# Block products over the whole depth in the second MLP product of a hybrid decoder, weight sums on GpSimd

## The reference

```python
hm = rms_norm(x, mlp_norm_g[l]) @ w_mlp1[l]      # 1024 -> 4096
x = x + jnp.square(jax.nn.relu(hm)) @ w_mlp2[l]  # 4096 -> 1024
```

## Time and profile before

| | us |
|---|---|
| median of 3 runs | 3008.79 (3005.19 to 3010.06) |
| the profiled execution | 3007.68 |
| its span, first to last instruction | 3005.6 |
| PE busy | 2824.3 (94%) |
| DVE busy | 1738.5 (58%) |
| POOL busy | 1596.1 (53%) |
| ACT busy | 1129.2 (38%) |
| mean granted clock of TensorE | 0.977 of 2.4 GHz |
| DMA | 208.27 MB, mean 69 GB/s |

### The profile page before, as it was taken

How to read it: one execution, slowest core, us unless ns; L and a number is a source line. 1 busy time by engine, 2 the same in 40 slices (tenths; PEclk the granted TensorE clock), 3 DMA queues, 4 the chain that set the end, 5 groups by cost and what they waited for, 6 DMA issues and landing times.

```text
span 3005.6 us, 33919 instructions
## 1 busy us (share of the span) xinstructions
PE 2824.3 (94%) x12958; PEld 2192.6 (73%) x12958; DVE 1738.5 (58%) x1775; ACT 1129.2 (38%) x1762; POOL 1596.1 (53%) x897
## 2 busy tenths in 40 slices
PE   8999999999999988888999999999999999888887
PEld 6766668887788877666787566788787888766665
DVE  8574465034733357989776644630446333598987
ACT  3455543242433333222215655422414333422233
POOL 4334433422577776666633345234136777766666
PEclk9999999999999999999999999999999999999999
DMA  3100011310133342222110000113011333423221
GB/s 130 47 14 1 15 43 49 106 56 28 45 110 113 113 140 98 70 98 84 56 55 33 14 1 15 56 57 112 29 39 60 109 111 110 146 78 105 70 98 56
DMA packets 96298, 208.27 MB, mean 69 GB/s; under 512 B 11280, under 2 KB 13328, under 8 KB 95504
## 3 DMA queue, kind: packets, MB, share of 16 engines
q1 hardware_dynamic: 96144, 206.18, 20.3%
HBM read 168.13 MB, written 38.01 MB: 69 GB/s over the span
## 4 chain that ended last, share of the span: by engine, by line
PE 65%; DVE 20%; POOL 7%; ACT 3%; issue 2%; DMA 2%; SPq 0%; DVEq 0%; POOLq 0%; ACTq 0%
PE ps L1018 16%; PE ps L1514 12%; PE ps L1588 9%; PE ps L1386 6%; DVE raw_b L2514 6%; DVE b_op L2510 5%; PE ps L1240 4%; POOL ring L887 3%; PE ps L1270 2%; POOL raw L893 2%; PE ps L1442 2%; PE ps L1605 2%; PE ps L1466 2%; PE ps L1256 2%; DVE z L2491 2%
## 5 line engine op out<-in xcount | busy, mean ns | idle before, releaser
L1588 PE MATMUL ps<-b_op,a_op 128*128 128x512 f32 x2352 | 579.8, 409 | 109.0 <-DVE x L2491 59.2
L1588 PEld LDWEIGHTS ps<-b_op,a_op 128*128 128x128 f32 x2352 | 464.8, 199 | 223.7 <-DVE x L2491 64.2
L1018 PE MATMUL ps<-hA,wsp 128*128 128x512 f32 x1920 | 443.1, 392 | 0.1
L721 POOL TENSOR_TENSOR wsp<-raw,ones 128x1024 fp32r<-128x1024 f32 x63 | 125.9, 1999 | 570.8 <-PE ps L1018 454.9
L1018 PEld LDWEIGHTS ps<-hA,wsp 128*128 128x128 f32 x1920 | 360.3, 188 | 80.9 <-issue 6.2
L922 POOL TENSOR_TENSOR a_op<-raw_a,a_op 128x1024 fp32r<-128x1024 f32 x102 | 282.7, 2772 | 224.6 <-ACT a_op L1989 217.0
L887 POOL TENSOR_TENSOR ring<-raw,ring 128x512 fp32r<-128x512 f32 x210 | 272.9, 1299 | 150.4 <-ACT ring L1949 140.9
L1514 PE MATMUL ps<-hT,ring 128*128 128x512 f32 x1440 | 337.3, 394 | 16.1 <-POOL ring L887 16.1
L1514 PEld LDWEIGHTS ps<-hT,ring 128*128 128x128 f32 x1440 | 273.0, 190 | 76.7 <-POOL ring L887 19.5
L1976 ACT ACTIVATE b_op<-raw_b 128x1024 fp32r<-128x1024 f32 x98 | 103.5, 1056 | 424.3 <-DVE raw_b L2514 279.3
L1514 PE MATMUL ps<-hB,ring 128*128 128x512 f32 x1080 | 250.2, 389 | 0.8 <-POOL ring L887 0.8
(11 more groups left out here) (326 smaller groups left out, 4592.4 us busy)
## 6 DMA issues: line engine op xcount, KB each, us to landing
raw<-in_weight_tiles SPq DMA_DIRECT2D x108, 512.0 KB, 3.3
hidden_tiles<-hm_s SPq DMA_DIRECT2D x128, 256.0 KB, 2.0
raw_a<-in_weight_tiles SPq DMA_DIRECT2D x64, 512.0 KB, 3.9
raw_b<-hidden_tiles SPq DMA_DIRECT2D x64, 512.0 KB, 5.4
raw<-in_weight_tiles SPq DMA_DIRECT2D x120, 256.0 KB, 3.1
outT<-x SPq DMA_DIRECT2D x16, 256.0 KB, 2.2
x<-in_xT SPq DMA_DIRECT2D x3, 1024.0 KB, 9.6
wh<-in_head_weights SPq DMA_DIRECT2D x8, 256.0 KB, 2.7
```

What stands on the lines that cost most here:

```text
L721: pool.tensor_tensor(wsp[:, s, 0, :], raw[:, s, :], ones[:, 0:1].to_broadcast([P, TILE]), ALU.mult).then_inc(w_ready[s], 1)
L1018: last = pe.matmul(ps[:, 2 * buf + half, 0:n], w[:, k, col:col + P], rhs(part, k, half * n, n), start=(at_k == 0 and w is w_hi and part == 0),
L1588: last = pe.matmul(ps[:, bank, :], w[:, part, q // 2, r, (q % 2) * P:(q % 2 + 1) * P], h[:, a, r, :], start=(r == 0 and part == 0 and a == ...
```

## The change

The loops of the second MLP product are turned around. A step n is product p = n // 8 and depth block s = n % 8; all eight depth blocks of one product are accumulated in four PSUM banks (M1, M7, M6, M3 in banks 4 to 7, the others in 0 to 3), the eighth block included, so nothing is plain any more and the accumulators `z` are gone. After each product DVE adds its four banks to the blocks of `x` that need it: 13 additions of 4 x 512 elements, and four of 512 after M3. The last two steps of M3 are done unit by unit, from two slots of their own.

The sums of hidden operands are made once, during the first MLP product, by DVE (`pair_sums`, four of 128 x 512 per iteration), and stored to DRAM ready for use: three plain quarters and four sums per pair. The weight operands are loaded anew for each product; eight of M1's stay in `kept_a` and are updated in place. Their sums (M7, M5, M6, M3) are made by POOL (`operand_sum`), one step ahead, between the lows. M5 loads a second weight block (`raw_c`). A weight load is now two transfers with runs of 256 elements. ACT puts two copies ahead of a root at the start of the first MLP product, and `mu` and the `hT` tiles lie elsewhere. Whatever waits are new stand in the diff, cut to its core:

```diff
+STEPS = NFB
+FILLS = NPR * STEPS
+RING_FILLS = FILLS - 2
+OPERAND_SUMS = (P_M7, P_M5, P_M6, P_M3)
...
-        slots = (A, A + 16 * K, A + 48 * K, B + 16 * K)
...
+        slots = (A + 16 * K, A + 48 * K, A, A + 32 * K, B + 8 * K, B + 24 * K)
...
+        raw_c = [at(f"raw_c{n}", B + (24 + 4 * n) * K, [P, 2, HT]) for n in range(4)]
...
+                    def store_sums(f):
+                        for j, p in enumerate((P_M7, P_M5, P_M6, P_M4)):
+                            sp.wait_ge(ht_sum, here(ht_sum, 4 * f + j + 1))
+                            sp.dma_start(hm_d[layer, f, p, :, :], hts[j][:, :]).then_inc(ht_st, 16)
...
+                    def load_weights(n):
+                        p, s = step(n)
+                        rows, parity = {P_M1: (0, 0), P_M2: (0, 1), P_M7: (1, 0), P_M5: (1, 0), P_M6: (1, 1), P_M4: (1, 1),
+                                        P_M3: (0, 1)}[p]
+                        load_block(kept_a[s] if p == P_M1 else raw_a[n % SLOTS], n, rows, parity)
+                        if p == P_M5:
+                            load_block(raw_c[n % SLOTS], n, 1, 1)
...
+                    def load_hidden(n):
+                        p, s = step(n)
+                        sp.dma_start(raw_b[n % SLOTS][:, :, :], hm_d[layer, 2 * s:2 * s + 2, p, :, :].rearrange("r p t -> p r t"))\
+                            .then_inc(ld_b[n % SLOTS], 16)
...
+                            sp.wait_ge(hm_st, here(hm_st, 48 * f))
+                            for n in range(2):
+                                load_weights(n)
+                                load_hidden(n)
+                        store_sums(f - 1)
+                        if more:
...
+                    for n in range(2, SLOTS):
+                        load_weights(n)
+                    sp.wait_ge(hm_st, here(hm_st, 48 * NFP))
+                    for n in range(2, SLOTS):
+                        load_hidden(n)
+                    store_sums(NFP - 1)
+                    sp.wait_ge(c_add, here(c_add, NPR * (NFP - 1)))
+                    for n in range(SLOTS, FILLS):
+                        sp.wait_ge(b_lo, here(b_lo, n - SLOTS + 1))
+                        load_hidden(n)
+                        sp.wait_ge(a_lo, here(a_lo, W1_FILLS + n - SLOTS + 1))
+                        if n == 6:
+                            sp.wait_ge(ht_st, here(ht_st, 64 * NFP))
+                        load_weights(n)
                     if last_layer:
                         sp.dma_start(fin_g[:, :], final_g).then_inc(fin_ld, 16)
...
-                    def a_add(b, n, out, x0, x1, op):
-                        pool.tensor_tensor(raw_a[out][:, :, :], raw_a[x0][:, :, :], raw_a[x1][:, :, :], op).then_inc(a_sum, 1)
...
+                    def operand_sum(n):
+                        p, s = step(n)
+                        pool.wait_ge(blk_ready[n % SLOTS], here(blk_ready[n % SLOTS], W1_LOADS + loads_a(n)))
+                        kept, new = kept_a[s][:, :, :], raw_a[n % SLOTS][:, :, :]
+                        if p == P_M5:
+                            pool.tensor_tensor(new, new, raw_c[n % SLOTS][:, :, :], ALU.add).then_inc(s_sum, 1)
+                            return
+                        pool.wait_ge(a_lo, here(a_lo, W1_FILLS + n - 2 * STEPS + 1))
+                        first, second = (kept, new) if p == P_M7 else (new, kept)
+                        pool.tensor_tensor(kept, first, second, ALU.subtract).then_inc(s_sum, 1)
...
-                    def fold(n, out, x0):
-                        pool.tensor_tensor(out[:, :, :], out[:, :, :], x0[:, :, :], ALU.add).then_inc(fold_z, 1)
...
+                    for n in range(FILLS):
+                        if n + 1 < FILLS and step(n + 1)[0] in OPERAND_SUMS:
+                            operand_sum(n + 1)
+                        operand_low(n)
...
+                    def operand_products(n, q):
+                        p, s = step(n)
+                        w = a_op[op_slot(n)].rearrange("p a c (r m) -> p a c r m", m=2 * P)
+                        h = b_op[op_slot(n)]
+                        for r in range(2):
+                            for part, a in ((0, 0), (0, 1), (1, 0)):
+                                last = pe.matmul(ps[:, 4 * (1 - p % 2) + q, :], w[:, part, q // 2, r, (q % 2) * P:(q % 2 + 1) * P],
+                                                 h[:, a, r, :], start=(s == 0 and r == 0 and part == 0 and a == 0),
+                                                 stop=(s == STEPS - 1 and r == 1 and part == 1))
+                        return last
...
+                    for n in range(RING_FILLS):
+                        p, s = step(n)
+                        operands_ready(n)
+                        if s == 0 and p == 0:
+                            pe.wait_ge(p1_kept, here(p1_kept, NFP - 1))
+                            pe.wait_ge(c_add, here(c_add, NPR * (NFP - 1) - 4))
+                            pe.wait_ge(hm_sq, here(hm_sq, 4 * NFP - 2))
+                        elif s == 0 and p == 1:
+                            pe.wait_ge(hm_sq, here(hm_sq, 4 * NFP))
+                        elif s == 0:
+                            pe.wait_ge(x_add, here(x_add, adds_before(p - 1)))
+                        for q in range(4):
+                            last = operand_products(n, q)
+                        last.then_inc(u_done, 1)
+                    operands_ready(FILLS - 1)
+                    for q in range(4):
+                        if last_layer and q == 2:
                             fin_means(0)
+                        for n in range(RING_FILLS, FILLS):
+                            last = operand_products(n, q)
+                        last.then_inc(u_done, 1)
                     if last_layer:
...
                     def hidden_sq(f, n, bank, k, half):
                         act.wait_ge(hm_t, here(hm_t, 4 * f + n + 1))
                         if f:
-                            act.wait_ge(hm_st, here(hm_st, 64 * f))
+                            act.wait_ge(hm_st, here(hm_st, 48 * f))
+                            act.wait_ge(ht_sum, here(ht_sum, 4 * f))
...
+                    def operands_high(n):
+                        p = step(n)[0]
+                        if n < SLOTS:
+                            act.wait_ge(p_done, here(p_done, NPR * (NFP - 2) + P_M7 + n + 1))
+                        elif n < RING_FILLS:
+                            act.wait_ge(u_done, here(u_done, n - SLOTS + 1))
...
+                    def pair_sums(f):
+                        dve.wait_ge(hm_sq, here(hm_sq, 4 * f + 4))
+                        if f:
+                            dve.wait_ge(ht_st, here(ht_st, 64 * f))
+                        b11, b12, b21, b22 = (hms[k][:, cols_of(half)] for k in range(2) for half in range(2))
+                        dve.tensor_tensor(hts[0][:, :], b22, b12, ALU.subtract).then_inc(ht_sum, 1)
+                        dve.tensor_tensor(hts[1][:, :], b12, b11, ALU.subtract).then_inc(ht_sum, 1)
+                        dve.wait_ge(ht_sum, here(ht_sum, 4 * f + 2))
+                        dve.tensor_tensor(hts[2][:, :], b22, hts[1][:, :], ALU.subtract).then_inc(ht_sum, 1)
+                        dve.wait_ge(ht_sum, here(ht_sum, 4 * f + 3))
+                        dve.tensor_tensor(hts[3][:, :], b21, hts[2][:, :], ALU.subtract).then_inc(ht_sum, 1)
...
-                    def b_sub(b, n, out, x0, x1):
-                        dve.tensor_tensor(raw_b[out][:, :, :], raw_b[x0][:, :, :], raw_b[x1][:, :, :], ALU.subtract).then_inc(b_sum, 1)
...
+                    def operand_low(n):
+                        op = b_op[op_slot(n)]
+                        dve.wait_ge(b_hi, here(b_hi, n + 1))
+                        dve.tensor_tensor(op[:, 1, :, :], raw_b[n % SLOTS][:, :, :], op[:, 0, :, :].bitcast(F32), ALU.subtract)\
                             .then_inc(b_lo, 1)
+                    c11, c12, c21, c22 = (x[:, 4 * (1 - rows):4 * (2 - rows), cols_of(half)] for rows in range(2) for half in range(2))
+                    X_BLOCKS = {P_M1: ((c11, 0), (c12, 0), (c21, 0), (c22, 0)), P_M2: ((c11, 1),), P_M7: ((c21, 3), (c22, 4)),
+                                P_M5: ((c12, 2), (c22, 7)), P_M6: ((c12, 8), (c21, 6), (c22, 9)), P_M4: ((c21, 11),)}
+                    def block_add(p, i):
+                        out, before = X_BLOCKS[p][i]
+                        bank = 4 * (1 - p % 2)
+                        dve.wait_ge(u_done, here(u_done, STEPS * (p + 1)))
+                        if before:
+                            dve.wait_ge(x_add, here(x_add, before))
+                        dve.tensor_tensor(out, ps[:, bank:bank + 4, :], out, ALU.add).then_inc(x_add, 1)
...
-                    def panel_adds(b, p, qs=range(4)):
-                        for q in qs:
-                            out = {P_M1: z1[:, q, :], P_M7: z7[:, q, :], P_M5: z5[:, q, :], P_M6: z6[:, q, :],
-                                   P_M4: x[:, 4 + q, 0:HT], P_M3: x[:, q, HT:T]}[p]
```

(29 more changed lines are left out.)

537 lines of the change are left out of this document (125 added, 412 removed).

## The result

The changed kernel takes 2923.03 us (median of 4 runs, 2921.71 to 2925.76), the kernel before beside it 3007.54 us: a ratio of 0.972, 95% interval 0.9703 to 0.9737. It is 84.5 us faster where 163 were forecast, and above the whole range of 2825 to 2882.

A forecast was written before the change was run, and what follows sets the result against it. VectorE was taken to bound the second MLP product. 3007.68 us less 87.0 (layer 0) and 90.9 (layer 1), plus 15 for the first product and 1.1 for the median, gave 2846; 80% range 2825 to 2882.

The forecast's parts named there:

- What bounds the kernel: The second MLP product is bound by VectorE's in-order list, not TensorE; 85 to 90 us of waits and low clock.
- parts 1 and 2: Second product: 1344 matmuls per layer, 304.7 us; VectorE at most 5.0 us per step against 5.44, so off the path.
- Part 3: Second product: GpSimd's heavy step takes 5.8 us against TensorE's 5.44, covered by four slots; 0 to 3 us per layer.
- Part 4: Between the two MLP products: loads of steps 2 and 3 come slightly late; charged 1 us, bounds 0 and 4.
- Part 5: Second product's loads: no loss per byte, share 0.58, in M5 0.87; 48 more stores at 0.43 us, nothing waiting closely.
- rival 3: Second product: transfers of 1 KB runs at double price, 9 to 20 us per layer, 2864 to 2886; chance 0.07.
- Part 6: First product: VectorE's sums delay M4, 0.45 us per period, 13 us; with the start +15, bounds -6 and +45.
- Rival 2: First product: port turns cost 1.5 us per period, 29 us more, 2875; chance 0.10.
- The start: First product's opening: early copies bring M7 some 3 us forward, sums put M4 back 4; costs 1 us per layer.
- The end: After the last product: four additions, squares and scaling as before, 14.3 us.
- What would be seen: Signs: second product 305 to 311 us, first product's periods 19.4 to 19.6; wrong if a period passes 20 us.
- rival 4: Second product paced by the latency of its loads, slower than before from 20 us landing time; 3070; chance 0.02.

The follow-up runs named there:

- e3: The changed kernel with all hidden sums made, but only those of the first two and the last pair stored (values wrong); 2865.8 us.
- e1: The changed kernel with the four stores of hidden sums moved behind the load of the second weight block in SP's list; 2872.71 us.
- e7: The changed kernel with two tiles in turn for weight block 1, its load issued earlier and the sum stores behind all four loads; 2844.06 us.
- e4: The changed kernel with ScalarE's old order at the start of the first MLP product restored, root ahead of weight copies; 2925.66 us.
- e5_seam: The changed kernel with step 2's hidden operand loaded ahead of step 3's weights, and the last pair's sums stored after step 4's loads; 2921.02 us.
- e10_all: e7 with the edits of e4 and e5_seam added, everything computed; 2832.19 us.

## Why the prediction was wrong, step by step

- **What bounds the kernel; parts 1 and 2: right.** The second product went to 311.2 and 312.3 us, against 307.7 and 308.7, with TensorE busy in 98% of it. The lows of hidden operands took 112.1 us in layer 0 and the block additions 29.7:

```profile
L2389 DVE TENSOR_TENSOR b_op<-raw_b,b_op 128x1024 fp32r<-128x1024 f32 x55 | 112.1, 2040 | 145.7 <-ACT b_op L1908 145.7
...
L2403 DVE TENSOR_TENSOR x<-ps,x 128x2048 f32<-128x2048 f32 x13 | 29.7, 2281 | 0.0
```

- **Part 3, GpSimd: right.** A heavy step in M5 and the next low, with what VectorE does beside them:

```profile
1290.04 2.41 POOL L917 TENSOR_TENSOR a_op<-raw_a,a_op 128x1024 fp32r<-128x1024 f32 x1
1290.99 2.53 DVE L2389 TENSOR_TENSOR b_op<-raw_b,b_op 128x1024 fp32r<-128x1024 f32 x1 [0.98 <-ACT b_op L1908]
1292.40 3.39 POOL L926 TENSOR_TENSOR raw_a<-raw_a,raw_c 128x1024 f32<-128x1024 f32 x1
1293.45 2.28 DVE L2403 TENSOR_TENSOR x<-ps,x 128x2048 f32<-128x2048 f32 x1
1295.75 2.39 POOL L917 TENSOR_TENSOR a_op<-raw_a,a_op 128x1024 fp32r<-128x1024 f32 x1
```

  1295.75 - 1290.04 = 5.71 us, against 5.8, and the lead of the slots covered the lag: no wait for `a_op` behind the seam. VectorE's low ends 1.1 us after GpSimd's instruction and GpSimd's sum waits for it. VectorE's addition at 1293.45, which has one operand in PSUM, runs at full speed through GpSimd's sum. The page SBUF — State Buffer of the Trainium skill ("SBUF: two separate sides") limits the lock to VectorE operations with two SBUF inputs or in a two-port mode; the trace agrees.
- **Part 4, the seam: the mechanism right, the term too small.** Charged 1 us, bounds 0 and 4; measured 4.9 and 4.8. The forecast let the transfers of steps 2 and 3 start at the seam. In the trace SP issues four weight transfers first, the hidden operand of step 2 comes at 1151.52 us, 4.4 after the seam, and takes 6.9 to land. What was not priced is the place in SP's list, the same omission as below. The 20 us around the wait also ran at a granted clock of 0.91.
- **Part 5, transfers: the step that failed.** "48 more x 0.43 us in SP's list, where nothing waits closely." The bytes and runs of the second product were judged rightly: the share was 0.57 from 1200 to 1255 us against 0.58, 0.81 from 1261 to 1305 us, where M5's blocks are loaded, against 0.87; no sign of rival 3. But of the stores, four per period were issued ahead of the last weight loads, and something did wait closely: the single tile of block 1. It was worth 57 us (e3), 50 of them by place alone (e1). What the sum lacks is the cycle through this tile: release by GpSimd, issue, landing, high, low. It took 22.36 us where the text allowed TensorE's 19.04 and 0.45 more.
- **Part 6, the first product: the price right, the path wrong.** VectorE's sums took 5.8 us (930.91 to 936.67) where 6.3 was forecast. With the load out of the cycle, the mean period behind the first is 19.23 us in e7 (layer 0) against 19.10 in before and 19.49 forecast. The step followed one period through ScalarE, VectorE, GpSimd and TensorE without any load in it, and so left out the one resource that the change loads most. It also charged the turns to the path through M4 alone, though they lengthen GpSimd's work by 1.05 us on the load's cycle. Rival 2 gave 1.5 us per period; measured were 3.1 more than before's 19.10. (Four sums alone are given as 2.6 us by halves of 1.21, which makes 2.4; nothing hangs on it, as the working takes 0.65 for each.)
- **The start, in the same part: the sign wrong.** M7 came 3.8 us later and not 3 sooner, since GpSimd's early lows take the port from VectorE's list. Mostly hidden here by the longer periods (e4).
- **The end: right.** 14.4 us from the last of the earlier trace rows to the end of the span, against 14.3.
- **What would be seen.** The text said that a period over 20 us would make it wrong; that is the line that fired. No rival had the cause: rival 4 had load latency, but in the second product and at 20 us.

## What to carry to other kernels

Before calling a store or a transfer free, find the buffer that has one tile only and add up its own loop, from the engine that releases it through the queue's position, the landing and the first consumer back to that engine; the slack of that loop, and not the mean load of the queue, is what new transfers may use. A loop that doesn't pass the bounding engine hardly shows in its list of waits while it is shorter than the engine's period (here some 0.5 us were left of 19). Look for the few waits that do show, in every layer: here in four of 28 periods of the kernel before, which were longer by up to 1.4 us. A gain made ahead of such a loop is worth something only once the loop is shortened, so open it first, by a second tile and an earlier load, and then try the small edits again.

## What the runs showed of the hardware

- A burst stretches the landing of a load at its end: 5.0 us for 256 KB with five other transfers still under way at its issue and 289 to 395 GB/s moving, against 3.7 in e1 without the stores ahead and 3.2 in before (medians over layer 0: 4.6, 3.9 and 3.3). The stores of `hm_s` landed in 3.4 rather than 2.0 us.
- At the seam, 20-us stretches ran at up to 379 GB/s with a DMA share near 1, the most that these traces show over such a time. A stretch of e5_seam in layer 1, then one of after in layer 0 (the granted clock is the third number from the end):

```profile
2597.00:2617.00 20.00, 18.45 (x82) 14.95 (x81) 11.78 (x13) 9.36 (x11) 11.57 (x4) 1.00 0.91 315
...
1157.00:1177.00 20.00, 15.09 (x61) 12.04 (x60) 12.28 (x6) 11.48 (x12) 15.72 (x5) 0.91 1.07 379
```

  In the first, TensorE waited 1.6 us and its granted clock stayed at 1.00 (2.4 GHz). Behind waits of 2.4 and 2.65 us (e10_all), 2.8 us (e5_seam, layer 0) and 4.9 us (after), 20-us stretches at the same place had 0.91, some of it at 1.2 GHz.
- A VectorE `hTf` operation of 512 elements took 0.74 us alone and 1.77 us beside a GpSimd instruction, and the list of 16 lasted 14.8 or 23.1 us by that alone (before, after).
- Periods that run on a load's cycle scatter: 21.4 to 22.8 us in one layer of after, and means of 22.24 to 22.55 in kernels that are alike in this stage, 3 us per layer. A small edit can't be judged by the total in such a kernel.
